# Sparse attention's compression ahead of the norms, four ada_w units at other steps, and 128 rows in the scan's decays product

## The chip, the cores and the metric

The kernel runs on one core of a Trainium2 chip, as one program. The metric is the device time of one execution in microseconds. Everything is computed in float32. A core has a matrix engine (TensorE, PE), a vector engine (VectorE, DVE), an engine for activations (ScalarE, ACT), a small general one (GpSimd, POOL) and SyncE (SP), whose queue issues the weight loads here. Each runs its own list of instructions in order, and they wait for each other by semaphores. Weights come from HBM by DMA into SBUF; TensorE writes into PSUM.

## What is computed

The reference is one block of a hybrid model (short convolution, native sparse attention, gated delta rule, then a two-level mixture of experts) followed by two blocks with modulation (MLA with a feed-forward part, a state-space mixer with a mixture of experts), for 256 tokens of width 1024. What matters here are three pieces of it:

```python
def nsa_compress(kv, pe, w1, w2):            # keys and values of the compressed branch
    idx = jnp.arange(n_cmp)[:, None] * CMP_STRIDE + jnp.arange(CMP_LEN)[None, :]
    blocks = kv[:, idx] + pe[:, None, :]
    flat = jnp.moveaxis(blocks, 3, 2).reshape(b, n_cmp, g, CMP_LEN * d)
    return jax.nn.gelu(flat @ w1) @ w2

q = rms_norm(u_q.reshape(b, s, g, hpg, d), qk_gain[0])
k_c = rms_norm(nsa_compress(kv[:, :, 0], ...), qk_gain[1])
k_s = rms_norm(kv[:, :, 2], qk_gain[2])
k_w = rms_norm(kv[:, :, 4], qk_gain[3])

mod = cond @ ada_w[i] + ada_b[i]             # modulation, 6144 columns for each of two layers

a_cs = jnp.cumsum(dt * a)                    # the scan: decays of 32 heads over the tokens
decay = jnp.exp(a_t[..., :, None] - a_t[..., None, :])
```

The compression takes the first 256 columns of the key and value projection as they are, without a norm. The modulation rows depend on nothing but `cond`, and the first layer's are used long after the attention.

## The kernel before

**Weights.** A weight matrix is cut into units of up to 2 MB (4096 columns of a [128, 4096] float32 tile). `Ring` holds four slots. SyncE issues the loads in the order in which the units were added, and a load waits until the unit four places before it is no longer needed (`emptied`). The order of `columns_unit`, `gate_unit`, `branch_unit` and `ada_units` in `block` is therefore the order of the DMA queue. An ada_w pair is two units, 4 MB, and gives 1024 columns of modulation.

**Split weights.** Most units are multiplied in three passes (high by high, high by low, low by high). `Split` cuts a unit into parts of [128, 1024]: ScalarE casts a part to its high half (`make_hi`, L192), VectorE subtracts it from the ring's to get the low half (`make_lo`, L202), TensorE multiplies (L257 to L259). There are four part buffers, so part n can be cast only when part n-4 has been multiplied. The last low half of a unit frees its ring slot. The ada_w and cmp units are multiplied straight from the ring, and TensorE frees them.

**PSUM.** Four pairs of banks are taken in turn (`banks.take`), each freed by whoever reads it out; `hold` keeps a pair out of the turn.

**The stages in question.** `gdn_*` is the delta rule, at whose end TensorE makes AU, then waits for VectorE's `o`, then transposes it (oT). `nsa_*` follows. Its TensorE list is: the products of the three nsa units (queries; 512 columns of keys and values; 256 more), ada_w pairs 3, 4 and 5, each a product of 64 matmuls (`ada_pe`, L1086) that ScalarE copies (`ada_act`), TensorE turns (`ada_turn_pe`) and VectorE stores (`ada_turn_dve`); then, when all the norms are done, the transposes of q (nqT) and keys (nkT); the transposes of dup (kcT), a doubled copy of the unnormed keys and values; then, from `fl` (the shifted blocks plus `cmp_pe`, 16 instructions of VectorE, L1803), the compression product of 128 matmuls (L1663), its gelu (h1, h2, h1T) and second product (kc), with steps of `gate (2,0)` between. Then `attention_pe` runs 12 jobs with more gate and branch steps beside them. When the stage is over (`finished(s, S["nsa"])` in `sync`), the first expert weights are issued.

VectorE in this stage: the low halves, `nsa_norm_dve` three times (squares, sums, a wait for GpSimd's power, two or three multiplications a half), dup (L1791), the ada stores, `fl`.

**The scan.** `csT` holds the running sums of 32 heads, one a row. For each head `decays_pe` (L3097) multiplies a column of `ident`, broadcast to 128, by `csT`, which puts row h on all 128 partitions. Two of them stand ahead of the loop of `ssm_pe` and one in each of its steps but the last two, in front of the step's part of the x or z projection.

Of the kernel before, what the change touches and what calls it, by code (L numbers as in the profile page):

```python
# [13 lines left out]
ACT = mybir.ActivationFunctionType  # L14
AX = mybir.AxisListType

P = 128
# [318 lines left out]
def block(nc, A, out):  # L336
# [5 lines left out]
    def sb(name, shape, dt=F32, where=None):  # L342
        return (where or ctx).enter_context(nc.sbuf_tensor(name, shape, dt))
# [247 lines left out]
    csT = sb("csT", [32, T], where=sm)  # L591
# [58 lines left out]
    def branch_unit(r, half):  # L650
        columns_unit(("branch", r, half), w_branch[r], 512 * half, 512, row_parts(512, 4))
# [5 lines left out]
    branch_unit(0, 1)  # L657
    columns_unit(("nsa", 0), w_in, O_Q, 512, row_parts(512))
    columns_unit(("nsa", 1), w_in, O_KV, 512, row_parts(512))
    columns_unit(("nsa", 2), w_in, O_KV + 512, 256, row_parts(256))  # L660
    gate_unit(2, 0)
    ada_units(0, 3, ADA_PAIRS)
# [3 lines left out]
    gate_unit(2, 1)  # L666
    branch_unit(2, 1)
# [596 lines left out]
    def gdn_pe(p):  # L1264
# [95 lines left out]
        ins.then_inc(*e.up("AU"))  # L1360
        p.wait_ge(*st.dve.of("o"))
# [3 lines left out]
    def gdn_act(a):  # L1365
# [49 lines left out]
        banks.empty(e, "ST")  # L1415

# [215 lines left out]
    def nsa_pe(p):  # L1632
# [12 lines left out]
        for h0 in (0, 4):  # L1645
            ps = banks.take(p, "nqT", h0)
            transposes(p, ps, [q[:, t, 64 * h:64 * h + 64] for h in range(h0, h0 + 4) for t in range(NT)]).then_inc(*e.up("nqT", h0))
        ps = banks.take(p, "nkT")
        transposes(p, ps, [kv[:, t, 256 + 256 * b + 64 * gr:256 + 256 * b + 64 * gr + 64]
                           for b in range(2) for gr in range(2) for t in range(NT)]).then_inc(*e.up("nkT"))  # L1650
# [16 lines left out]
        ada_turn_pe(p, 0, 5)  # L1667
        merge_step_pe(p, 2, 0)
# [3 lines left out]
        merge_step_pe(p, 2, 1)  # L1672
# [17 lines left out]
    def nsa_act(a):  # L1690
# [11 lines left out]
        for n in range(3, ADA_PAIRS):  # L1702
            ada_act(a, 0, n)
# [7 lines left out]
        a.wait_ge(*st.pe.of("kcT"))  # L1711
        a.copy(kcT[:, :, :].rearrange("p h t -> p (h t)"), banks.of("kcT")).then_inc(*e.up("kcT"))
        banks.empty(e, "kcT")
        a.wait_ge(*st.pe.of("cmp"))
        a.copy(h1, banks.of("cmp")[:, 0:P]).then_inc(*e.up("h1"))
        banks.empty(e, "cmp")
        merge_step_act(a, 2, 0)
        a.wait_ge(*st.dve.of("h2"))
        a.activation(h2, h2, ACT.Sigmoid, scale=2.0 * math.sqrt(2.0 / math.pi)).then_inc(*e.up("h2"))
        a.wait_ge(*st.pe.of("h1T"))  # L1720
        a.copy(h1T[:, :, :].rearrange("p n c -> p (n c)"), banks.of("h1T")[:, 0:P]).then_inc(*e.up("h1T"))
        banks.empty(e, "h1T")
# [13 lines left out]
        merge_step_act(a, 2, 3)  # L1736
        attention_act(a, st, nsa_s, nsa_pT, nsa_mx, nsa_den, 1.0, nsa_jobs, beside=merge_beside_act)
# [4 lines left out]
    def nsa_norm_dve(v, buf, c0, n, gain, scale, k0):  # L1742
# [5 lines left out]
        for t in range(NT):  # L1748
            settle(v, v.tensor_reduce(rn[:, t, k0:k0 + n], w[:, t, :].rearrange("p (n d) -> p n d", d=64), AX.X, ADD),
                   d, "squares", k0)  # L1750
        v.wait_ge(*st.pool.of("rn", k0))
# [26 lines left out]
    def nsa_dve(v):  # L1778
# [13 lines left out]
        ada_turn_dve(v, 0, 3)  # L1792
        ada_turn_dve(v, 0, 4)
# [11 lines left out]
        ada_turn_dve(v, 0, 5)  # L1805
# [4 lines left out]
        merge_step_dve(v, 2, 0)  # L1810
# [9 lines left out]
        attention_dve(v, st, nsa_s, nsa_mx, nsa_den, 1.0, nsa_jobs, nsa_score, nsa_finish, beside=merge_beside_dve)  # L1820
        v.wait_ge(*st.act.of("ynT"))
# [1207 lines left out]
    def ssm_pe(p):  # L3029
# [18 lines left out]
        for t in range(NT):  # L3048
            ins = p.transpose(ps[:, t * 32:t * 32 + 32], csT[:, t * P:(t + 1) * P], ident[0:32, 0:32])
# [253 lines left out]
    def ssm_dve(v):  # L3303
# [23 lines left out]
        v.memset(on32[:, :], 1.0).then_inc(*d.up())  # L3327
        v.memset(upad2[:, :, :, 0:3], 0.0).then_inc(*d.up("pad"))
# [4 lines left out]
        v.tensor_tensor_scan(csT[:, :], on32[:, :], daT[:, :], 0.0, MUL, ADD).then_inc(*d.up("csT"))  # L3333
# [257 lines left out]
```

## Time and profile before

| | |
|---|---|
| median of 3 runs | 2529.43 us (2526.84 to 2530.2) |
| profiled execution | 2528.53 us, its span 2526.7 us |
| TensorE busy | 2146.5 us, 85% of the span |
| VectorE, ScalarE busy | 1424.3 us (56%), 1157.9 us (46%) |
| DMA | 656.69 MB, mean 260 GB/s |
| mean cast of a part (L192), mean low half (L202) | 1015 ns, 1178 ns |

The profile is one execution with the start and end of each instruction. It is read here in these ways: the chain of work that ended last (who held whom up), the timeline (instructions in order; in brackets the idle time ahead and who ended it), windows (busy time of each engine in a stretch, granted TensorE clock as a share of 2.4 GHz, DMA), waits, and the DMA issues. A float32 matmul appears as two passes or more, and the ends of matmuls are modelled, so distances between starts are the safer measure. In a group of the timeline the second number is its whole length.

### The profile page before, as it was taken

What the parts mean: (1) busy time and instruction counts of PE and PEld (TensorE: products, weight loads), DVE (VectorE), ACT (ScalarE), POOL (GpSimd) and SP (SyncE); (2) the same over time, 40 slices, a digit from 0 to 9 for tenths busy, and PEclk for the clock granted to TensorE, in tenths of its full rate; (3) what the DMA queues carried; (4) which work ended last, traced back from release to release, by engine and by line L of the source; (5) the groups of instructions that cost most, each with busy time, mean ns of one, the idle gap of its engine ahead of it and who ended that gap; (6) DMA issues with size and microseconds to landing.
All of it is one profiled execution on the core that took longest, in us unless ns stands there. A gap on an engine that the chain in (4) does not pass through costs nothing.

```text
span 2526.7 us, 29676 instructions
## 1 busy us (share of the span) xinstructions
PE 2146.5 (85%) x12223; PEld 1622.4 (64%) x12223; DVE 1424.3 (56%) x1976; ACT 1157.9 (46%) x1520; POOL 40.9 (2%) x107
## 2 busy tenths in 40 slices
PE   6889788876656656887999988879999999999997
PEld 6867566652111111566997867668787787887875
DVE  3844435421111101434455666658889888888997
ACT  4432244310000000443443556538777787777775
POOL 0000100000000000000000000000000000000000
PEclk9989898879888888997999888889999999999999
DMA  8451651469999999476445322238989989989994
GB/s 265 167 182 69 234 199 56 178 253 408 409 409 409 409 409 402 165 267 234 151 183 183 112 90 99 84 125 293 362 323 329 373 324 359 339 314 371 332 335 189
DMA packets 267692, 656.69 MB, mean 260 GB/s; under 512 B 13456, under 2 KB 38548, under 8 KB 267546
## 3 DMA queue, kind: packets, MB, share of 16 engines
q1 hardware_dynamic: 266592, 652.90, 69.6%
q8 instruction: 101, 1.65, 0.3%
q10 hardware_dynamic: 952, 1.77, 0.2%
q14 instruction: 47, 0.37, 0.0%
HBM read 653.60 MB, written 1.05 MB: 259 GB/s over the span
## 4 chain that ended last, share of the span: by engine, by line
PE 68%; DMA 16%; DVE 9%; ACT 4%; issue 2%; POOL 0%; ACTq 0%; DVEq 0%; POOLq 0%; SPq 0%
PE psum L257 17%; PE psum L258 17%; PE psum L259 16%; PE psum L252 9%; DMA ring<-in_w_expert_up 5%; DMA ring<-in_w_expert_down 5%; DMA ring<-in_w_expert_gate 5%; PE psum L2344 2%; DVE w_lo L202 2%; PE psum L1086 1%; ACT w_hi L192 1%; PE psum L879 1%; PE psum L2366 1%; DMA ring<-in_ada_w 1%; DVE xbc L885 1%
## 5 line engine op out<-in xcount | busy, mean ns | idle before, releaser
L202 DVE TENSOR_TENSOR w_lo<-ring,w_hi 128x1024 fp32r<-128x1024 f32 (+1 forms) x778 | 905.0, 1178 | 399.7 <-ACT w_hi L192 384.6
L192 ACT CAST w_hi<-ring 128x1024 fp32r<-128x1024 f32 (+1 forms) x778 | 785.2, 1015 | 442.9 <-PE psum L259 438.6
L257 PE MATMUL psum<-w_hi,xg_hi 128*128 128x512 f32 (+1 forms) x768 | 294.7, 384 | 1.3 <-ACT xg_lo L2027 1.3
L259 PE MATMUL psum<-w_lo,xg_hi 128*128 128x512 f32 (+1 forms) x768 | 289.5, 377 | 0.0
L258 PE MATMUL psum<-w_hi,xg_lo 128*128 128x512 f32 (+1 forms) x768 | 289.5, 377 | 0.0
L2344 PE MATMUL psum<-ring,hT 128*32 128x512 f32 x960 | 149.7, 756 | 114.6 <-DMA ring<-in_w_expert_gate 64.8
L2344 PEld LDWEIGHTS psum<-ring,hT 128*32 128x32 f32 x960 | 29.8, 126 | 229.4 <-issue 79.0
L257 PEld LDWEIGHTS psum<-w_hi,xg_hi 128*128 128x128 f32 x768 | 144.8, 189 | 31.1 <-issue 1.7
L258 PEld LDWEIGHTS psum<-w_hi,xg_lo 128*128 128x128 f32 x768 | 144.9, 189 | 29.4 <-issue 1.7
L259 PEld LDWEIGHTS psum<-w_lo,xg_hi 128*128 128x128 f32 x768 | 144.7, 188 | 29.2
L257 PE MATMUL psum<-w_hi,midT_hi 128*128 128x512 f32 x352 | 140.8, 400 | 3.9 <-DVE w_lo L202 3.9
L2196 DVE TENSOR_TENSOR x<-x,psum 128x1024 f32<-128x1024 f32 x14 | 17.1, 1221 | 218.8 <-PE psum L252 218.8
L258 PE MATMUL psum<-w_hi,midT_lo 128*128 128x512 f32 x352 | 139.5, 396 | 0.0
L259 PE MATMUL psum<-w_lo,midT_hi 128*128 128x512 f32 x352 | 139.5, 396 | 0.0
L2366 PE MATMUL psum<-ring,midT 128*32 128x512 f32 x480 | 71.4, 727 | 40.5 <-DMA ring<-in_w_expert_down 40.0
L257 PE MATMUL psum<-h_f_hi,w_hi 128*128 128x256 f32 x352 | 99.1, 282 | 2.0 <-DVE h_f_lo L802 2.0
L258 PE MATMUL psum<-h_f_hi,w_lo 128*128 128x256 f32 x352 | 98.9, 281 | 0.0
L259 PE MATMUL psum<-h_f_lo,w_hi 128*128 128x256 f32 x352 | 98.9, 281 | 0.0
L257 PEld LDWEIGHTS psum<-w_hi,midT_hi 128*128 128x128 f32 x352 | 66.3, 188 | 20.8 <-issue 5.4
L2379 ACT COPY midT<-psum 128x512 f32<-128x512 f32 x8 | 4.7, 585 | 161.5 <-PE psum L879 161.5
L259 PEld LDWEIGHTS psum<-w_lo,midT_hi 128*128 128x128 f32 x352 | 66.3, 188 | 16.1
L258 PEld LDWEIGHTS psum<-w_hi,midT_lo 128*128 128x128 f32 x352 | 66.3, 188 | 15.4
(662 smaller groups left out, 3722.7 us busy)
## 6 DMA issues: line engine op xcount, KB each, us to landing
ring<-in_moe_w_gate SPq DMA_DIRECT2D x40, 2048.0 KB, 9.3
ring<-in_moe_w_up SPq DMA_DIRECT2D x40, 2048.0 KB, 10.0
ring<-in_moe_w_down SPq DMA_DIRECT2D x40, 2048.0 KB, 9.2
ring<-in_w_expert_gate SPq DMA_DIRECT2D x30, 2048.0 KB, 17.5
ring<-in_w_expert_up SPq DMA_DIRECT2D x30, 2048.0 KB, 17.6
ring<-in_w_expert_down SPq DMA_DIRECT2D x30, 2048.0 KB, 17.8
ring<-in_ada_w SPq DMA_DIRECT2D x24, 2048.0 KB, 8.9
ring<-in_ssm_w_in SPq DMA_DIRECT2D x10, 2048.0 KB, 8.0
```

Of the source, the lines that this page charges most:

```text
L192: a.copy(self.buffers(n, src.shape)[0], src).then_inc(*self.hi_made.up())
L202: v.tensor_tensor(lo, src, hi.bitcast(F32), SUB).then_inc(*self.lo_made.up())
L252: ins = p.matmul(o, l, r, start=n == 0, stop=n == len(terms) - 1)
L257: p.matmul(o, l[0], r[0], start=start, stop=False)
L258: p.matmul(o, l[1], r[0], start=False, stop=False)
L259: return p.matmul(o, l[0], r[1], start=False, stop=stop)
L879: ins = p.transpose(ps[0:c, n * P:n * P + r], src, ident[0:r, 0:r])
L885: settle(v, v.scalar_tensor_tensor(out_, padded[:, f, j:j + T], w_cols(j), out_, MUL, ADD), st.dve, *name)
L1086: ins = p.matmul(ps[32 * quarter:32 * quarter + 32, 0:256], cond[:, k:k + 1].to_broadcast([P, 32]), w[quarter // 2][:, k, c0:c0 + 256], st ...
L2196: v.tensor_tensor(M.acc[:, t, :], M.acc[:, t, :], run.banks.of(st.name, "scatter", i, t), ADD).then_inc(*st.dve.up("acc", i, t))
L2344: ins = p.matmul(ps[slots_of(j), g * 512:(g + 1) * 512], M.xg[:, 2 * q + k, slots_of(j)], w[:, j, k, :], start=2 * q + k == 0, stop=2 * q ...
L2366: ins = p.matmul(ps[slots_of(j), cut], M.midT[:, q, slots_of(j)], w[:, j, cut], start=q == 0, stop=q == 3)
```

## The change

In the order of units, ada_w pair 3 is loaded ahead of nsa 0, pair 4 ahead of nsa 2, and pair 5 behind gate (2,1). TensorE multiplies pair 3 between AU and oT at the end of `gdn_pe`, pair 4 between nsa 0 and nsa 1, and pair 5 just ahead of the attention jobs; they are turned behind nsa 0, behind kcT, and behind the jobs. On TensorE kcT and the compression product come ahead of the transposes of q and the keys, gate step (2,0) ahead of the compression product and (2,1) behind it. On ScalarE the copies of kcT, h1 and h1T come ahead of those of nqT and nkT. On VectorE the squares are split off the norms (`nsa_squares_dve`) and done between low halves as soon as their columns are there, dup comes ahead of all norms, and the norms of the two keys come behind `fl`; the norm of q stays ahead of it. In the scan, `csT` has 128 rows, set to zero first, and the decays product takes all 128 of them.

```diff
-    csT = sb("csT", [32, T], where=sm)
+    csT = sb("csT", [P, T], where=sm)
@@ order of units
+    ada_units(0, 3, 4)
     columns_unit(("nsa", 0), w_in, O_Q, 512, row_parts(512))
     columns_unit(("nsa", 1), w_in, O_KV, 512, row_parts(512))
+    ada_units(0, 4, 5)
     columns_unit(("nsa", 2), w_in, O_KV + 512, 256, row_parts(256))
     gate_unit(2, 0)
-    ada_units(0, 3, ADA_PAIRS)
     for j in range(2):
         columns_unit(("cmp", j), A["cmp_w1"][0][j], 0, 256)
     branch_unit(2, 0)
     gate_unit(2, 1)
+    ada_units(0, 5, ADA_PAIRS)
     branch_unit(2, 1)
@@ gdn_pe
         ins.then_inc(*e.up("AU"))
+        ada_pe(p, 0, 3)
         p.wait_ge(*st.dve.of("o"))
@@ gdn_act, at its end
+        ada_act(a, 0, 3)
@@ nsa_pe
-        ada_pe(p, 0, 3)
-        ada_pe(p, 0, 4)
-        ada_turn_pe(p, 0, 3)
-        ada_pe(p, 0, 5)
-        ada_turn_pe(p, 0, 4)
-        p.wait_ge(*st.dve.of("normed"))
...
+            if n == 0:
+                ada_turn_pe(p, 0, 3)
+                ada_pe(p, 0, 4)
         p.wait_ge(*st.dve.of("dup"))
         ps = banks.take(p, "kcT")
...
+        ada_turn_pe(p, 0, 4)
+        merge_step_pe(p, 2, 0)
         p.wait_ge(*st.dve.of("fl"))
...
-        ada_turn_pe(p, 0, 5)
-        merge_step_pe(p, 2, 0)
+        merge_step_pe(p, 2, 1)
         p.wait_ge(*st.dve.of("h1"))
         ps = banks.take(p, "h1T")
         transposes(p, ps, [h1]).then_inc(*e.up("h1T"))
-        merge_step_pe(p, 2, 1)
+        p.wait_ge(*st.dve.of("normed"))
+        for h0 in (0, 4):
+            ps = banks.take(p, "nqT", h0)
...
         merge_step_pe(p, 2, 3)
+        ada_pe(p, 0, 5)
         p.wait_ge(*st.act.of("vc"))
         attention_pe(p, st, nsa_s, nsa_pT, nsa_jobs, beside=merge_beside_pe)
+        ada_turn_pe(p, 0, 5)
@@ nsa_act: ada_act(0, 4) behind the copy of nsa 0, ada_act(0, 5) ahead of attention
@@ nsa_dve
-        for n in range(3):
-            split.make_lo(v, min(split.end(unit["nsa", n]) + PARTS, cap))
-        v.wait_ge(*st.act.of("proj", 2))
-        nsa_norm_dve(v, q, 0, 8, gains[:, 0, :], 64.0 ** -0.5, 0)
-        nsa_norm_dve(v, kv, 256, 2, gains[:, 2, :], 1.0, 8)
-        nsa_norm_dve(v, kv, 512, 2, gains[:, 3, :], 1.0, 10)
+        split.make_lo(v, min(split.end(unit["nsa", 1]) + 1, cap))
+        v.wait_ge(*st.act.of("proj", 0))
+        ada_turn_dve(v, 0, 3)
+        nsa_squares_dve(v, q, 0, 8, 0)
+        split.make_lo(v, min(split.end(unit["nsa", 1]) + PARTS, cap))
+        v.wait_ge(*st.act.of("proj", 1))
         for jg in range(4):
             for c in range(2):
                 v.tensor_copy(dup[:, jg, :, 64 * c:64 * c + 64], kv[:, :, 64 * jg:64 * jg + 64]).then_inc(*d.up("dup"))
+        nsa_squares_dve(v, kv, 256, 2, 8)
+        split.make_lo(v, min(split.end(unit["nsa", 2]) + PARTS, cap))
+        nsa_norm_dve(v, q, 0, 8, gains[:, 0, :], 64.0 ** -0.5, 0)
...
+        v.wait_ge(*st.act.of("proj", 2))
+        nsa_squares_dve(v, kv, 512, 2, 10)
+        merge_step_dve(v, 2, 0)
+        ada_turn_dve(v, 0, 4)
+        nsa_norm_dve(v, kv, 256, 2, gains[:, 2, :], 1.0, 8)
+        nsa_norm_dve(v, kv, 512, 2, gains[:, 3, :], 1.0, 10)
@@ decays_pe
-        product(p, ps[:, 0:T], [(ident[0:32, h:h + 1].to_broadcast([32, P]), csT[:, :])]).then_inc(*S["ssm"].pe.up("decay", h))
+        product(p, ps[:, 0:T], [(ident[:, h:h + 1].to_broadcast([P, P]), csT[:, :])]).then_inc(*S["ssm"].pe.up("decay", h))
@@ ssm_dve
+        v.memset(csT[:, :], 0.0).then_inc(*d.up())
...
-        v.tensor_tensor_scan(csT[:, :], on32[:, :], daT[:, :], 0.0, MUL, ADD).then_inc(*d.up("csT"))
+        v.tensor_tensor_scan(csT[0:32, :], on32[:, :], daT[:, :], 0.0, MUL, ADD).then_inc(*d.up("csT"))
```

## Rows read from the trace of the kernel before

**Rows 1.** The page, chain that ended last, share of the span by engine

```profile
PE 68%; DMA 16%; DVE 9%; ACT 4%; issue 2%; POOL 0%; ACTq 0%; DVEq 0%; POOLq 0%; SPq 0%
```

**Rows 2.** Timeline of TensorE, end of gdn to compression: start, length, instructions, [idle before]

```profile
248.75 2.05 PE L252 MATMUL psum<-shared,decT 128*128 128x128 f32 x16 [0.78 <-DVE shared L1478]
258.13 1.97 PE L879 MATMUL psum<-ident,shared 128*128 128x128 f32 x8 [7.32 <-DVE shared L1489]
...
289.24 3.66 PE L1086 MATMUL psum<-ring,cond 128*32 128x256 f32 x64
299.71 5.39 PE L1086 MATMUL psum<-ring,cond 128*32 128x256 f32 x64 [6.82 <-DMA ring<-in_ada_w]
...
311.77 6.18 PE L1086 MATMUL psum<-ring,cond 128*32 128x256 f32 x64 [6.13 <-DMA ring<-in_ada_w]
...
318.35 1.92 PE L879 MATMUL psum<-ident,q 128*64 128x128 f32 x16
...
328.35 6.43 PE L1663 MATMUL psum<-ring,fl 128*32 128x128 f32 x128 [6.34 <-DVE fl L1803]
```

**Rows 3.** Windows: stretch, length, busy PE, PEld, DVE, ACT, POOL (count), clock, DMA, GB/s

```profile
297.60:301.40 3.80, 1.69 (x17) 0.93 (x21) 3.61 (x6) 0.00 (x0) 0.00 (x0) 0.50 1.05 386
328.30:334.70 6.40, 6.35 (x128) 5.74 (x128) 0.00 (x0) 0.00 (x0) 0.00 (x0) 0.56 0.25 92
335.20:350.80 15.60, 15.25 (x66) 10.06 (x65) 5.31 (x10) 5.71 (x13) 0.72 (x2) 1.00 0.89 309
351.00:465.00 114.00, 102.58 (x501) 78.96 (x501) 60.63 (x169) 57.15 (x137) 0.00 (x0) 0.90 0.17 59
575.00:1010.00 435.00, 268.03 (x1643) 79.42 (x1635) 61.17 (x174) 19.48 (x31) 0.35 (x2) 0.85 1.03 408
```

**Rows 4.** SyncE's DMA issues; last, ada_w's size and median us to landing

```profile
211.14 0.37 SPq L139 DMA_DIRECT2D ring<-in_w_in  x1
...
265.56 30.55 SPq L139 DMA_DIRECT2D ring<-in_ada_w  x6
...
464.89 0.92 SPq L128 DMA_DIRECT2D place_ns<-in_w_expert_gate  x2
...
ring<-in_ada_w SPq DMA_DIRECT2D x6, 2048.0 KB, 9.0
```

**Rows 5.** Timeline of VectorE, the filling of fl

```profile
323.19 5.10 DVE L1803 TENSOR_TENSOR fl<-kcT,cols 64x120 f32<-64x120 f32 x16 [4.42 <-ACT kcT L1712]
```

**Rows 6.** Timeline of ScalarE, first cast of nsa 0 and the copies of nqT

```profile
222.76 1.04 ACT L192 CAST w_hi<-ring 128x1024 fp32r<-128x1024 f32 x1 [0.90 <-PE psum L259]
...
319.42 1.91 ACT L1706 COPY hT<-psum 64x1024 f32<-64x1024 f32 x2 [0.47 <-PE psum L879]
```

**Rows 7.** Timeline of TensorE, from kcT2 to the first scores

```profile
345.19 0.21 PE L1680 MATMUL psum<-ident,kc 30*64 30x30 f32 x1 [0.35 <-DVE kc L1817]
...
350.83 1.06 PE L252 MATMUL psum<-kcT,hT 64*128 64x15 f32 x8
```

**Rows 8.** Timeline of TensorE in the first experts

```profile
582.70 3.24 PE L2344 MATMUL psum<-ring,hT 128*32 128x512 f32 x16 [3.19 <-DMA ring<-in_w_expert_gate]
588.44 1.92 PE L2344 MATMUL psum<-ring,hT 128*32 128x512 f32 x16 [2.51 <-DMA ring<-in_w_expert_gate]
```

**Rows 9.** Timeline of TensorE in the scan; last, a wait of its weight loads

```profile
1449.95 2.78 PE L252 MATMUL psum<-xbc 128*128 128x256 f32 x16
1452.48 0.47 PE L257 MATMUL psum<-w_hi,h_ssm_hi 128*128 128x512 f32 x1
...
1480.11 0.69 PE L252 MATMUL psum<-csT,ident 32*128 32x256 f32 x2
1480.74 0.39 PE L257 MATMUL psum<-h_ssm_hi,w_hi 128*128 128x256 f32 x1
...
PEld psum L257 <- issue: 7.9, 22, 0.7
```

**Rows 10.** Timeline of VectorE, the memset of 32 rows

```profile
1413.62 0.27 DVE L3327 MEMSET on<- 32x256 f32 x1
```

More of the change, by code:

```diff
@@ L1638, in nsa_pe @@
             by_token_pe(p, u, h_mix, [[ps[:, t * 512:t * 512 + w] for t in range(NT)]])
-        ada_pe(p, 0, 3)
-        ada_pe(p, 0, 4)
-        ada_turn_pe(p, 0, 3)
-        ada_pe(p, 0, 5)
-        ada_turn_pe(p, 0, 4)
-        p.wait_ge(*st.dve.of("normed"))
[L1645 to L1650, printed above, removed]
+            if n == 0:
+                ada_turn_pe(p, 0, 3)
+                ada_pe(p, 0, 4)
         p.wait_ge(*st.dve.of("dup"))
@@ L1671, in nsa_pe @@
         transposes(p, ps, [h1]).then_inc(*e.up("h1T"))
-        merge_step_pe(p, 2, 1)
+        p.wait_ge(*st.dve.of("normed"))
+        for h0 in (0, 4):
+            ps = banks.take(p, "nqT", h0)
+            transposes(p, ps, [q[:, t, 64 * h:64 * h + 64] for h in range(h0, h0 + 4) for t in range(NT)]).then_inc(*e.up("nqT", h0))
+        ps = banks.take(p, "nkT")
+        transposes(p, ps, [kv[:, t, 256 + 256 * b + 64 * gr:256 + 256 * b + 64 * gr + 64]
+                           for b in range(2) for gr in range(2) for t in range(NT)]).then_inc(*e.up("nkT"))
         p.wait_ge(*st.act.of("h1T"))
@@ L1701, in nsa_act @@
             banks.empty(e, "unit", u)
-        for n in range(3, ADA_PAIRS):
-            ada_act(a, 0, n)
+            if n == 0:
+                ada_act(a, 0, 4)
+        a.wait_ge(*st.pe.of("kcT"))
+        a.copy(kcT[:, :, :].rearrange("p h t -> p (h t)"), banks.of("kcT")).then_inc(*e.up("kcT"))
+        banks.empty(e, "kcT")
+        merge_step_act(a, 2, 0)
+        a.wait_ge(*st.pe.of("cmp"))
+        a.copy(h1, banks.of("cmp")[:, 0:P]).then_inc(*e.up("h1"))
+        banks.empty(e, "cmp")
+        a.wait_ge(*st.dve.of("h2"))
+        a.activation(h2, h2, ACT.Sigmoid, scale=2.0 * math.sqrt(2.0 / math.pi)).then_inc(*e.up("h2"))
+        a.wait_ge(*st.pe.of("h1T"))
+        a.copy(h1T[:, :, :].rearrange("p n c -> p (n c)"), banks.of("h1T")[:, 0:P]).then_inc(*e.up("h1T"))
+        banks.empty(e, "h1T")
         for h0 in (0, 4):
@@ L1710, in nsa_act @@
         banks.empty(e, "nkT")
[L1711 to L1722, printed above, removed]
         merge_step_act(a, 2, 1)
@@ L1736, in nsa_act @@
         merge_step_act(a, 2, 3)
+        ada_act(a, 0, 5)
         attention_act(a, st, nsa_s, nsa_pT, nsa_mx, nsa_den, 1.0, nsa_jobs, beside=merge_beside_act)
@@ L1740, in nsa_act, with nsa_squares_dve @@
         a.copy(ys_[0][:, :, :].rearrange("p f t -> p (f t)"), banks.of("ynT")).then_inc(*e.up("ynT"))
-    def nsa_norm_dve(v, buf, c0, n, gain, scale, k0):
+    def nsa_squares_dve(v, buf, c0, n, k0):
         st = S["nsa"]
@@ L1750, in nsa_norm_dve @@
                    d, "squares", k0)
+    def nsa_norm_dve(v, buf, c0, n, gain, scale, k0):
+        st = S["nsa"]
+        d = st.dve
+        heads = buf[:, :, c0:c0 + 64 * n]
         v.wait_ge(*st.pool.of("rn", k0))
@@ L1791, in nsa_dve @@
                 v.tensor_copy(dup[:, jg, :, 64 * c:64 * c + 64], kv[:, :, 64 * jg:64 * jg + 64]).then_inc(*d.up("dup"))
-        ada_turn_dve(v, 0, 3)
-        ada_turn_dve(v, 0, 4)
+        nsa_squares_dve(v, kv, 256, 2, 8)
+        split.make_lo(v, min(split.end(unit["nsa", 2]) + PARTS, cap))
+        nsa_norm_dve(v, q, 0, 8, gains[:, 0, :], 64.0 ** -0.5, 0)
         v.memset(fl[:, :, :, 30:32], 0.0).then_inc(*d.up("fl"))
@@ L1804, in nsa_dve @@
                                         pe_cols.unsqueeze(2).to_broadcast([64, 8, 15]), ADD).then_inc(*d.up("fl"))
-        ada_turn_dve(v, 0, 5)
+        v.wait_ge(*st.act.of("proj", 2))
[4 more added lines that the diff above has]
+        nsa_norm_dve(v, kv, 512, 2, gains[:, 3, :], 1.0, 10)
         v.wait_ge(*st.act.of("h1"))
@@ L1809, in nsa_dve @@
         v.tensor_tensor(h2, h2, h1, MUL).then_inc(*d.up("h2"))
-        merge_step_dve(v, 2, 0)
         v.wait_ge(*st.act.of("h2"))
@@ L1820, in nsa_dve @@
         attention_dve(v, st, nsa_s, nsa_mx, nsa_den, 1.0, nsa_jobs, nsa_score, nsa_finish, beside=merge_beside_dve)
+        ada_turn_dve(v, 0, 5)
         v.wait_ge(*st.act.of("ynT"))
@@ L3048, in ssm_pe @@
         for t in range(NT):
-            ins = p.transpose(ps[:, t * 32:t * 32 + 32], csT[:, t * P:(t + 1) * P], ident[0:32, 0:32])
+            ins = p.transpose(ps[:, t * 32:t * 32 + 32], csT[0:32, t * P:(t + 1) * P], ident[0:32, 0:32])
         ins.then_inc(*e.up("cs"))
```

## The prediction

> **What bounds the kernel now.** I read the page first. The chain that ended last is mostly TensorE (68%), with DMA second (16%) [rows 1]; so a change pays only where TensorE stands still or works at length on that chain. The change touches two places, and I read each as a timeline, engine by engine.
>
> The first is the sparse-attention stage. Behind oT (258.13) TensorE multiplies the three nsa units and is through at 289.24. Then it does little for 46 us: it waits 6.82 and 6.13 us for ada_w to land, works on both at a low clock, waits another 6.34 us for VectorE to fill `fl`, and runs the compression product at 0.56 of full clock [rows 2, 3]. The cause shows in the DMA issues: all six ada_w units are issued from 265.56 on, in one block [rows 4], and the cmp units stand behind them. VectorE meanwhile does everything ahead of `fl`: squares and norms of q and both keys (q's norm is the stretch of 3.8 us at 297.6 [rows 3]), then dup, up to 310.3, and only then `fl` at 323.19, 5.1 us long [rows 5]. `fl` also waited for kcT, which was transposed behind nqT and nkT, whose copies ScalarE makes first [rows 2, 6]. Attention starts at 350.83 [rows 7].
>
> Is what is gained here kept? The first expert weights are issued at 464.89 [rows 4], when the stage is over, and the experts then run at the pace of DMA: TensorE waits 3.19 and 2.51 us before one quarter unit and another, and the stretch from 575 to 1010 moves 408 GB/s [rows 3, 8]. That stream is started by the end of the attention stage and by what follows it, and nothing in it has a time of its own. An earlier end shifts all of it, one for one.
>
> The second place is the state-space scan. There one step of about 4.28 us is 24 matmuls, 6 small ones and one decays product, with no gap of TensorE between them. This product (two passes, 32 rows) begins at 1480.11 and the next matmul at 1480.74: 0.63 us [rows 9].
>
> **The change, part by part, sparse attention.** I lay the new order out in the times of the trace of before.
>
> ada unit pair 3 goes in between AU (from 248.75, 2.05 us) and oT (258.13), where TensorE sat idle for 7.32 us [rows 2]. At full clock such a product of 64 matmuls is 3.66 us, at low clock up to 6.18 [rows 2]; either fits, so it costs nothing; without that cover it would cost 3.7. The idle left is 3.5 us. Gaps of 3.19 us were followed by a slow quarter, gaps of 2.51 by a fast one [rows 8], so I credit no clock gain to the next stage. Its weights take the ring places in front of nsa 0 and 1, so nsa 0 is now issued when nsa 2 was, at 211.14 [rows 4], and nsa 1 one unit later. nsa 0 is first cast at 222.76, and a 2 MB unit of ada_w took 9.0 us to land beside others [rows 6, 4]: 2.6 us of slack, counted as nothing.
>
> Nsa 0 ends at 272.2 (my reading from its 48 matmuls, 289.24 less 5.8 and 11.2). Behind it come turn 3 (0.5) and ada pair 4 (3.7), loaded from 255 on into an idle queue. So nsa 1 ends at 287.6 and nsa 2 at 293.4, 4.2 later than now. The casts of ScalarE and its copy that empties the bank of nsa 0 both fall under ada 4.
>
> VectorE: the squares of q, dup and the squares of the first keys now lie in the gaps between the w_lo parts (one of 1.2 us to each 2.8 us of TensorE) while nsa 1 and 2 are multiplied. The last part of gate (2,0) can be cast only when nsa 2 is done: a cast and a w_lo of the page's mean, 1.0 and 1.2 (table above) with the hand-overs, give 295.8. Then q's norm, still ahead of `fl`: 3.8, 299.6. kcT is transposed at 293.4, copied by 296.1, so no wait. `fl` 5.2 with its hand-over: done at 304.9. It was 328.3 [rows 2]: **23.4 us earlier**. TensorE does kcT (0.9), turn 4 and gate step (2,0) (2.8) in that time and then idles 7 us, so I leave the compression product at its slow 6.4 us [rows 2]: done at 311.3.
>
> From there: gate step (2,1) 2.8 (12 matmuls of 512 columns at 0.23), h1T 0.3, nqT and nkT 2.6 (moved in here; from 318.35 to 320.97 before [rows 2]), kc 0.8: 317.8. Gate step (2,2) ends at 320.6. ScalarE must first copy h1T, nqT twice and nkT (1.0 each [rows 6]), so the cast of step 1 is at 318.1 to 319.2, then the kc copies, the next cast, its w_lo on VectorE to 322.1, and kc's norm to 322.7: TensorE idles 2.1 us, a new wait (0.35 before [rows 7]). From kcT2 to the first scores 5.64 us, as before (345.19 to 350.83) [rows 7]: 328.4. Then ada pair 5, put before attention: its loads are issued when the compression product frees their slots, at 311.3, and take two units of at most 9 us each in the worst case, 5.1 at the stream's rate; landed by 323 or, at the outside, 330. At the full clock that TensorE had here from 335.2 to 350.8 [rows 3], 3.7: **scores start at 332.1, 18.7 us earlier.** If it runs at low clock, or lands last, 16.
>
> In the attention itself nothing else is added. gate (1,0) now needs the slot of gate (2,1), freed some 13 us into attention, and by 9 us a unit lands about 22 us in, just when its first part was to be cast; ScalarE has over 2 us to spare there. I count 0, with 2 us as the far end. Turn 5 (0.5) and its copy fall where TensorE waits for yn. The order in which the PSUM banks turn is the same in attention, shifted by one. So the stage brings -18.7 us; ends -12 (2 us each lost at nsa 0, `fl` and gate (1,0)) and -23.
>
> **The scan.** The rows 32 to 127 that are added are zeros in csT, and ident is zero there in the columns used, so the result is unchanged and the number of instructions too. What a 128-row pair of this shape costs is to be seen in cb's product: 16 passes, 8 of 256 columns and 8 of 128, in 2.53 us from 1449.95 to 1452.48, with no gap to the next matmul [rows 9]. That is 0.21 for a pass of 256, 0.42 a pair, against 0.63: 0.2 us saved per decays product. The weight loads tell why: after a decays pair the next load stood 0.36 us (22 times, 7.9 in all) for nothing that the profile shows [rows 9]. There are 32 products; 30 stand in the loop, and some 22 to 24 of them in stretches where TensorE has no gap. 23 x 0.2 = **-4.5 us**. Ends: 0, and 32 x 0.25 = -8. The memset adds some 0.3 us to VectorE (the 32-row `on` took 0.27 [rows 10]) where it waits for ScalarE's casts anyway, nothing on the path.
>
> The Trainium skill has two rules that pull apart here. Its page "TensorE: Matmul & The Clock Gate", section "Why this matters for your kernels", says that a single matmul of 32 rows takes the same time as one of 128; by that the padding brings nothing. Its page "TensorEngine Tiling (Array Packing)", section "Key Properties", says that a change of the tiling mode drains the engine; by that each decays product in a stream of 128-row matmuls pays twice. The row of 0.63 against 0.42 stands with the second.
>
> Sum: 18.7 + 4.5 = 23.2. The profiled execution took 2528.5 us with a span of 2526.7; less 23.2 it is 2505.3. The median of the runs shown is 2529.4, 0.9 above, so I predict 2506.2.
>
> **The rivals.** (a) *The padding brings nothing*, because the wait is in the weights and not in the rows: 2529.4 - 18.7 = 2510.7. For: the load before the pair is short already. Against: the 0.63. (b) *A wait takes the place of part of the gain in attention*: `fl` comes later than I lay it out, because VectorE is now asked for more between nsa 1 and nsa 2, or ada 5 lands late behind the compression product. 5 to 9 us lost: 2511 to 2515. (c) *More is gained*: the compression product at full clock (-2.5), no new wait at kcT2 (-2), fewer slow matmuls at 260 and 300: 2498 to 2501. (d) *Slower*: the two idle gaps close together (7 us at 297.6, 2.1 us at 320.6) leave TensorE at 1.2 GHz into attention, where before it ran at 2.4 GHz from 335.2 to 350.8 and at a mean of 0.91 through attention [rows 3]. A 512-column matmul takes 0.43 instead of 0.23; the stage from 351 to 465 has 102.6 us of TensorE work, so all of it at the lower level costs over 50 us, and from half of it on the change is slower: 2506 + 30 = 2536 for a little over half. Against: gaps of 2.5 us left the clock alone [rows 8], and after a wait of 6.34 us and the compression product TensorE had its full clock back at 335.2 [rows 3]. (e) *No change*: the gain stops at the expert stream; it would need a DMA that starts by itself, and none does: 2529.
>
> **How the numbers follow.** The forecast 64%, (a) 10%, (b) 12%, (c) 7%, (d) 4%, (e) 3%. The forecast's own range is 2501 to 2510. To hold 8 in 10 the range takes in (a), most of (b) and part of (c): 2498 to 2515. A measurement tells 0.2%, 5 us, from no change; faster 0.93, same 0.03, slower 0.04.
>
> **What would show it.** Right: AU followed by 64 ada matmuls and no ada_w wait of TensorE after 289; `fl` done near 305; one wait of about 7 us ahead of the compression product; scores from 332; the first expert issue near 446; decays pairs followed by the next matmul after 0.42 us. Wrong: a DMA wait in ada 5 or a ScalarE wait for gate (1,0), a granted clock under 0.8 between 325 and 350, or decays pairs still 0.63.

## The result and the profile after

The changed kernel takes **2493.67 us** (median of 4 runs, 2492.2 to 2503.84), the kernel before beside it 2529.81 (4 runs): a ratio of 0.9867, 95% interval 0.9839 to 0.9895. Two later comparisons gave 0.987 and 0.988; over all three its 12 runs have a median of 2495.6 us (2492.05 to 2503.97). The forecast was 2506.2 with a range down to 2498. The sign and the two mechanisms held, and more was gained than I allowed for: 2493.67 lies below the range. The profiled execution took 2494.8 us, its span 2493.1: 33.6 less than before.

The page's chain of the changed kernel by engine. DMA fell from 16% to 15% [rows 1], and TensorE's two waits for ada_w in this stage are gone:

```profile
PE 67%; DMA 15%; DVE 10%; ACT 5%; issue 2%; POOL 0%; ACTq 0%; DVEq 0%; POOLq 0%
```

Timeline of TensorE in the changed kernel, the lines that answer to [rows 2, 7]. (After's line numbers: L1086 is L1088 now, L879 L881, L1663 L1660, L1680 L1682.)

```profile
249.16 2.05 PE L252 MATMUL psum<-shared,decT 128*128 128x128 f32 x16 [0.78 <-DVE shared L1482]
251.15 3.66 PE L1088 MATMUL psum<-ring,cond 128*32 128x256 f32 x64
258.54 1.27 PE L881 MATMUL psum<-ident,shared 128*128 128x128 f32 x8 [3.74 <-DVE shared L1493]
...
272.67 3.66 PE L1088 MATMUL psum<-ring,cond 128*32 128x256 f32 x64
...
304.73 6.50 PE L1660 MATMUL psum<-ring,fl 128*32 128x128 f32 x128 [7.11 <-DVE fl L1814]
...
314.18 1.91 PE L881 MATMUL psum<-ident,q 128*64 128x128 f32 x16
...
322.22 0.21 PE L1682 MATMUL psum<-ident,kc 30*64 30x30 f32 x1 [1.58 <-DVE kc L1832]
...
327.87 3.66 PE L1088 MATMUL psum<-ring,cond 128*32 128x256 f32 x64
331.46 1.06 PE L252 MATMUL psum<-kcT,hT 64*128 64x15 f32 x8
```

The three ada_w products run at full clock, 3.66 us each, with no wait in front. The compression product starts at 304.73 instead of 328.35, the scores at 331.46 instead of 350.83. The queue of SyncE, and VectorE's and ScalarE's lines in the same place:

```profile
254.87 0.99 SPq L139 DMA_DIRECT2D ring<-in_ada_w  x2
...
311.30 0.99 SPq L139 DMA_DIRECT2D ring<-in_ada_w  x2
...
444.77 0.92 SPq L128 DMA_DIRECT2D place_ns<-in_w_expert_gate  x2
```
```profile
299.64 5.03 DVE L1814 TENSOR_TENSOR fl<-kcT,cols 64x120 f32<-64x120 f32 x16
```
```profile
315.25 1.92 ACT L1722 COPY hT<-psum 64x1024 f32<-64x1024 f32 x2 [0.61 <-PE psum L881]
...
319.48 1.03 ACT L192 CAST w_hi<-ring 128x1024 fp32r<-128x1024 f32 x1
```

`fl` has no wait in front any more (4.42 us for kcT before [rows 5]). Its end is set by VectorE's own work, with q's norm as the last piece of it. The first expert issue is 20.1 us earlier than before [rows 4].

The scan, timeline of TensorE, and the waits of the weight loads in the same stretch, to be set beside [rows 9]:

```profile
1459.58 0.78 PE L252 MATMUL psum<-xs,hT 128*128 128x64 f32 x6
1460.20 0.65 PE L252 MATMUL psum<-csT,ident 128*128 128x256 f32 x2
1460.50 0.47 PE L257 MATMUL psum<-h_ssm_hi,w_hi 128*128 128x256 f32 x1
```
```profile
PEld psum L257 <- issue: 1.5, 1, 1.5
```

From the start of the decays pair to the next matmul it is 0.30 us, where it was 0.63, and of the 22 unexplained waits of the weight loads one is left.

**Where the time went.** I cut both executions at the same instructions (starts of TensorE's matmuls, and the issue of the first expert weights), and took the lengths between. These are differences of starts in the timelines, not lines of the profile:

| stretch, us | before | after | difference |
|---|---|---|---|
| start to the first expert issue | 464.9 | 444.8 | -20.1 |
| to the first expert matmul | 83.4 | 77.5 | -5.9 |
| first experts, to MLA | 464.9 | 467.2 | +2.3 |
| MLA and feed-forward, to the first decays product | 445.1 | 445.5 | +0.4 |
| scan | 161.4 | 154.3 | -7.1 |
| scan's end to the second experts | 83.3 | 80.1 | -3.2 |
| to the end | 823.7 | 823.7 | 0 |

The two edited places give 27.2 us. The other 6.4 come from stretches in which the change altered nothing but the small memset of csT on VectorE, in the fourth. The forecast had 23.2 for the two places and nothing for the rest. Not every stretch is as steady as its row: over all profiles the scan, with one and the same code in it, took either 161.3 to 161.5 or 163.4 to 163.6 us with 32 or 64 rows, and either 154.1 to 154.6 or 156.4 with 128.

### The profile page after: what moved, and what is told of

It is laid out like the page before. It is cut to its first block, busy times and chain, and to the rows that moved or that the text cites. A ratio compares the mean times of both kernels' runs of the same rounds, so it can differ in the third digit from the quotient of the medians.

```text
span 2493.1 us, 29680 instructions
## 1 busy us (share of the span) xinstructions
PE 2128.2 (85%) x12223; PEld 1615.8 (65%) x12223; DVE 1424.0 (57%) x1977; ACT 1158.1 (46%) x1520; POOL 43.5 (2%) x107
## 4 chain that ended last, share of the span: by engine, by line
PE 67%; DMA 15%; DVE 10%; ACT 5%; issue 2%; POOL 0%; ACTq 0%; DVEq 0%; POOLq 0%
PE psum L257 17%; PE psum L259 16%; PE psum L258 16%; PE psum L252 8%; DMA ring<-in_w_expert_down 5%; DMA ring<-in_w_expert_up 5%; DMA ring<-in_w_expert_gate 5%; PE psum L2360 2%; DVE w_lo L202 2%; ACT w_hi L192 1%; PE psum L1088 1%; PE psum L2382 1%; PE psum L881 1%; DVE xbc L887 1%; PE psum L2071 1%
## 5 line engine op out<-in xcount | busy, mean ns | idle before, releaser
L257 PEld LDWEIGHTS psum<-w_hi,xg_hi 128*128 128x128 f32 x768 | 144.8, 188 | 31.1 <-issue 1.7
L258 PEld LDWEIGHTS psum<-w_hi,xg_lo 128*128 128x128 f32 x768 | 144.8, 189 | 29.4 <-issue 1.7
```

Source lines behind the costliest of these rows:

```text
L257: p.matmul(o, l[0], r[0], start=start, stop=False)
L258: p.matmul(o, l[1], r[0], start=False, stop=False)
```

## The experiments

None of the kernels leaves out or alters a part of the computation. Two theories stood at the start: **clock** (the two halves of the change are worth some 19 and 7 to 9 us, they add, and what is left over is TensorE's granted clock, which differs from one execution to the next in stretches that nobody edited) and **strengthening** (an earlier attention stage really makes what follows faster, so that the whole is more than its parts). Beside them: whether the attention edits need each other, and what the padding of the decays product pays for.

**1 and 2. Each half alone.** The attention edits with the old scan, and the scan's edit with the old attention:

```diff
# attention only: everything of the change but
-    csT = sb("csT", [P, T], where=sm)
+    csT = sb("csT", [32, T], where=sm)
-        product(p, ps[:, 0:T], [(ident[:, h:h + 1].to_broadcast([P, P]), csT[:, :])]) ...
+        product(p, ps[:, 0:T], [(ident[0:32, h:h + 1].to_broadcast([32, P]), csT[:, :])]) ...
# scan only: the kernel before with the four edits of csT, decays_pe, ssm_dve and the transposes of csT
```

> The changed kernel with the scan put back to 32 rows; the attention part is whole. By my ledger of the two traces the scan's loop brings 7 to 9 us (0.33 us for each of some 25 decays products), so this should take 2501 to 2503 us. By the prediction's price of 0.2 us a product it would be 2498. The first expert weights should be issued at 444.8 us, as in the changed kernel. If the 5.8 us that the stretch from that issue to the first expert matmul gained (83.4 to 77.6 us) belongs to the kernel's timing, it is 77.6 again here, since everything ahead of it is the same; if the clock there falls out differently at each execution, it will differ.

> The kernel before with the scan part of the change alone. Ledger: 7 to 9 us less, 2521 to 2523; by the prediction's price 4.5 less, 2525; by 'a matmul of 32 rows costs what one of 128 costs', no change. From the start of a decays pair to the next matmul 0.30 us instead of 0.62, and 0.33 less from step to step.

Measured: attention alone 2511.27 us (2505.91 to 2513.5), ratio 0.9929 [0.9912, 0.9945]; the scan alone 2519.71 (2517.22 to 2522.77), ratio 0.9961 [0.9947, 0.9975]. That is 17.8 and 9.3 us less than the 2529.04 of before beside them; the sum, 27.1, is 9 short of the 36.1 between the medians of the first comparison. Attention alone took 8 us more than the 2501 to 2503 expected, the scan alone a little less than its 2521 to 2523. The scan alone has its stretch at 154.2 us, 7.2 shorter, like the whole. Attention alone issues the first expert weights at 442.3, as early as the whole, but has 83.4 us from there to the first expert matmul, as before. Up to the scan its code is that of the changed kernel, which took 77.5.

**3 and 4. The two attention edits apart.** First the new order of the norms, kcT and `fl`, with the six ada_w units left in one block; then the ada_w units spread, with the old order:

```diff
# order only
-    ada_units(0, 3, 4)
     columns_unit(("nsa", 0), w_in, O_Q, 512, row_parts(512))
...
     gate_unit(2, 0)
+    ada_units(0, 3, ADA_PAIRS)
# spread only: the ada_w units as in the change, and in nsa_pe
+        p.wait_ge(*st.dve.of("normed"))
+        ... nqT, nkT ahead of kcT, and in nsa_dve the three whole norms ahead of dup
```

> The changed order inside the stage (kcT and the compression product ahead, squares early), but all three ada_w pairs loaded and multiplied in one block behind the nsa units, as before; scan as before. If the two edits need each other: TensorE comes to kcT only when pair 5 has landed, near 318.5 us, fl is ready near 325.5 (before 328.3), and what is moved behind the compression product takes that back, so 1 to 3 us less than before, 2527 to 2529. If each edit brings its own part, about 10 us less, 2520.

> The ada_w pairs at the new places in the queue and on TensorE, but norms, nqT and nkT ahead of kcT and the compression as before; scan as before. If the two edits need each other: nothing waits for ada_w any more, but the chain of norms and copies now sets the end; fl near 323.5 us, then ada pair 5 (3.7 us) ahead of attention, so 1 to 3 us less than before, 2527 to 2529. If each edit brings its own part, about 10 us less, 2520.

Measured: 2525.8 us for the order alone, ratio 0.9986 [0.9971, 1.0], and 2525.27 for the spread alone, 0.9987 [0.9976, 0.9999]. Some 3 to 4 us each by the medians, with intervals that touch or nearly touch no change (at the first expert issue of their profiles 3.0 and 0.7 us), where the two together bring 18 to 20. Both came out a little under the 2527 to 2529 expected if the two need each other, and well above the 2520 expected if each brings its own part. Timeline of TensorE, order alone:

```profile
300.11 5.34 PE L1086 MATMUL psum<-ring,cond 128*32 128x256 f32 x64 [6.93 <-DMA ring<-in_ada_w]
312.01 6.21 PE L1086 MATMUL psum<-ring,cond 128*32 128x256 f32 x64 [6.02 <-DMA ring<-in_ada_w]
325.99 3.70 PE L1658 MATMUL psum<-ring,fl 128*32 128x128 f32 x128 [3.06 <-DVE fl L1810]
```

and spread alone:

```profile
312.69 3.62 PE L881 MATMUL psum<-ident,q 128*64 128x128 f32 x16 [19.52 <-DVE kv L1762]
324.44 6.42 PE L1666 MATMUL psum<-ring,fl 128*32 128x128 f32 x128 [6.27 <-DVE fl L1809]
340.82 0.21 PE L1682 MATMUL psum<-ident,kc 30*64 30x30 f32 x1 [0.35 <-DVE kc L1822]
```

With the block left in place the two DMA waits stay. With it gone, and the norms still first, TensorE stands idle for 19.52 us behind VectorE: the transfers had hidden VectorE's work, and VectorE's work the transfers. Whoever removes one finds the other.

**5. The whole again,** on another chip, for its own scatter.

> The changed kernel itself once more, beside the kernel before. If the two parts simply add and the rest of what its first profile showed (5.8 us between the first expert issue and the first expert matmul, 3.2 us behind the scan) is the granted clock of that execution, its median is that of the attention part alone less 9.3 us: 2499 to 2504, with single runs from 2492 up, and a profile may show 83.4 us again in that stretch. If the two parts strengthen each other, 2492 to 2495 again.

Measured: 2495.25 us (2492.05 to 2500.35), ratio 0.987 [0.9851, 0.9889]; in its profile 77.5 us from the first expert issue to the first expert matmul, as in the first. That is under the 2499 to 2504 that the clock theory had asked and close to the 2492 to 2495 of strengthening; experiments 9 to 11 take the question up again.

**6. 64 rows in place of 128,** to learn whether the padding pays by the number of rows or by bringing the product into the shape of its neighbours.

```diff
-    csT = sb("csT", [P, T], where=sm)
+    csT = sb("csT", [64, T], where=sm)
-        product(p, ps[:, 0:T], [(ident[:, h:h + 1].to_broadcast([P, P]), csT[:, :])]) ...
+        product(p, ps[:, 0:T], [(ident[0:64, h:h + 1].to_broadcast([64, P]), csT[:, :])]) ...
```

> The changed kernel with csT and the decays product at 64 rows instead of 128. If what 32 rows cost is a switch of the array's shape between neighbouring matmuls, 64 rows cost the same: 0.62 us from a decays pair to the next matmul, 4.2 to 4.3 us a step. If it goes by the number of rows, the pair lies between, near 0.5 us. If only 32 rows are slow, 0.30 us.

Timeline of TensorE in the scan with 64 rows:

```profile
1461.59 0.69 PE L252 MATMUL psum<-csT,ident 64*128 64x256 f32 x2
1462.22 0.38 PE L257 MATMUL psum<-h_ssm_hi,w_hi 128*128 128x256 f32 x1
```

It is 0.63 us again, as with 32 rows, the weight loads have their 22 unexplained waits of 7.9 us in all back, and the scan's stretch is 161.5 us. One execution took 2509.93 us, within the range of the attention edits alone. So doubling the rows bought nothing, and filling all 128 bought everything. The price does not go by the row; it fits one paid where products of a part of the rows stand among products of all of them, which is a reading and not shown by itself: no run puts two such products side by side at full clock, or tries another number of rows.

**7. q's norm behind `fl`.** In the changed kernel q's norm, 3.8 us, is the last thing ahead of `fl` and on the path.

```diff
         split.make_lo(v, min(split.end(unit["nsa", 2]) + PARTS, cap))
-        nsa_norm_dve(v, q, 0, 8, gains[:, 0, :], 64.0 ** -0.5, 0)
...
         nsa_norm_dve(v, kv, 512, 2, gains[:, 3, :], 1.0, 10)
+        nsa_norm_dve(v, q, 0, 8, gains[:, 0, :], 64.0 ** -0.5, 0)
```

> The changed kernel with the norm of q (3.8 us of VectorE) behind fl and the keys' norms too. fl begins at 296 us instead of 299.7 and is ready at 301; TensorE's wait ahead of the compression product falls from 7.1 to 3.3 us. If VectorE is what sets this stretch, the scores start 3 to 4 us earlier, near 328, and the time falls by as much. If the norm then comes late for nqT behind the compression product, the gain is under 1.5 us.

Measured: 2493.47 us (2487.37 to 2499.61), ratio 0.9846 [0.9829, 0.9864], against 0.987 [0.9851, 0.9889] for the change on that chip; the intervals overlap. Timeline of TensorE:

```profile
302.39 5.00 PE L1660 MATMUL psum<-ring,fl 128*32 128x128 f32 x128 [3.60 <-DVE fl L1813]
...
311.66 0.33 PE L881 MATMUL psum<-ident,nsa_s 128*128 128x128 f32 x1 [1.27 <-DVE nsa_s L1827]
...
319.86 0.21 PE L1682 MATMUL psum<-ident,kc 30*64 30x30 f32 x1 [1.57 <-DVE kc L1832]
```

The wait in front of the compression product is 3.60 instead of 7.11. The product itself ran partly at full clock here and took 5.00 us, not 6.50, but 1.27 us of new wait follow it: h1's gelu stands behind q's norm on VectorE. In experiment 12, with the same order, the product took 6.46 us and this wait is missing; the two make up for each other. The scores are at 329.1, 2.4 us earlier, where 3 to 4 were expected.

**8. Work for TensorE in its gaps.** Between the attention and the experts TensorE stands still three times for longer (4.43, 6.12 and 6.67 us in the first profile); behind the last two it works mostly at the lower clock (in the kernel before 0.61 in the mean of the 34.9 us ahead of the first expert matmul, both gaps among them). Four, six and six matmuls of 512 columns on constants, whose results nobody reads, go into these gaps (`warm_pe`, called in `proj_pe` and twice in `moe1_pe`):

```diff
+        ps = banks.take(p, "warm", name)
+        for n in range(times):
+            ins = p.matmul(ps[:, 0:512], ident[:, :], ones[:, 0:1].to_broadcast([P, 512]), start=True, stop=True)
+        ins.then_inc(*st.pe.up())
+        banks.empty(st.pe, "warm", name)
```

> The changed kernel with matmuls that compute nothing of use in three gaps of TensorE between attention and the experts (4, 6 and 6 of 512 columns, each some 0.9 us at full clock, in gaps of 4.4, 6.1 and 6.7 us). If the two lengths of that stretch, 83.4 and 77.6 us, differ by when the clock falls and comes back in those gaps, it is 77.6 us or less in every profile, and the median is 3 to 8 us under that of the changed kernel. If the gaps have nothing to do with it, the median is the same or later by what the added matmuls stick out.

Measured: 2491.32 us (2486.13 to 2495.16), ratio 0.9842 [0.9827, 0.9858], 3.9 us under the change on that chip, with intervals that overlap. The stretch to the first expert matmul is 76.3 us, 1.2 less than in the best of the other executions.

**9 to 12. The whole and its halves once more, side by side,** and both tries in one kernel. They decide between the two theories, which the first eight had left open.

> The changed kernel once more, on the same chip and in the same rounds as its two halves below. Theory 'the halves add, and the granted clock decides the rest': the three kernels have the same code between the attention and the scan as each other's parts, so the time saved here is the sum of the savings of the two halves to within 3 us. Theory 'the halves strengthen each other': the saving stays 8 us above the sum, here 35 us against 18 and 9. Both expect 2492 to 2497 us for this kernel; the halves tell.

> The attention edits alone again (the scan's decays as in the kernel before). If the halves add: about 2503 (35 less 9 for the scan: a saving of 26), and in its profile the stretch from the placement's issue to the first expert matmul is 77.6 us rather than 83.4. If they strengthen each other: 2511 again (a saving of 18), with 83.4 us in that stretch.

> The scan edit alone again. 23 products that save 0.33 us each are 7.6 us. If nothing else is in it, 2521 to 2523, with the stretch before the second expert stage at 83.3 us; with that stretch at 80.1 us, 3 us less, 2518 to 2520. Both theories expect a saving of 7 to 11 us.

> Both tries in one kernel: q's norm stands behind fl and the key norms on VectorE, and 4, 6 and 6 matmuls on constants fill three gaps of TensorE between the attention and the experts. Nothing of the computation is left out. Scores 3 us earlier by the first (about 329), the stretch from the placement's issue to the first expert matmul 76.3 to 77.6 by the second. If both are real and add: 2487 to 2490, against 2493 to 2495 for the changed kernel on the same chip. If the granted clock alone made each of them, 2491 to 2495.

| on one chip | us, median | runs | ratio |
|---|---|---|---|
| before | 2529.05 (2523.95 to 2533.76) | 12 | |
| the change | 2497.91 (2495.59 to 2503.97) | 4 | 0.988 [0.9861, 0.9899] |
| attention alone | 2509.03 (2501.25 to 2515.18) | 6 | 0.9918 [0.99, 0.9936] |
| scan alone | 2519.64 (2517.16 to 2522.38) | 6 | 0.9965 [0.9953, 0.9976] |
| both tries | 2488.66 (2484.73 to 2491.4) | 5 | 0.9837 [0.9823, 0.9851] |

Here the halves save 20.0 and 9.4 us, and the whole 31.1: a sum of 29.4, apart by 1.7, well inside the scatter of the runs. Over all chips the medians are 2495.6 (12 runs), 2509.8 (10), 2519.65 (11) and 2529.2 (45 of before): 33.6 against 19.4 + 9.6 = 29.0. On the one chip the whole, at 2497.91, is a microsecond above the 2492 to 2497 that both theories had expected. The whole and the attention alone scatter by 4.3 us from run to run (standard deviation), so the 4.6 between are about two of their uncertainty (4.3 us over the root of 12, and of 10, are 1.2 and 1.4). By the means instead of the medians the whole saves 32.8 and the halves 20.3 + 9.8 = 30.1, and 2.7 are left. Attention alone also had the longer scan, 163.4 and 163.6 us against 161.4 before, in both of its profiles; that is 2 us outside its edits. **Strengthening is not needed, though a few microseconds of it are not excluded.** My guess for attention alone, 2503, missed; 83.0 us stood in the stretch for which the clock theory had asked 77.6. That theory is right in that either length occurs with the same code, and was wrong in tying it to the change.

The profiles show it directly. First the same code, the change, in two executions: windows (stretch, length, busy PE, PEld, DVE, ACT, POOL with counts, granted clock, DMA share, GB/s) of the first profile,

```profile
322.50:335.00 12.50, 12.50 (x101) 7.71 (x100) 2.02 (x7) 4.43 (x15) 0.00 (x0) 1.00 0.35 126
335.00:400.00 65.00, 61.00 (x295) 46.09 (x293) 39.29 (x108) 34.31 (x88) 0.00 (x0) 0.95 0.36 130
400.00:445.00 45.00, 37.41 (x194) 29.77 (x194) 20.27 (x57) 21.52 (x41) 0.00 (x0) 0.83 0.14 47
```

and of experiment 9:

```profile
322.50:335.00 12.50, 12.50 (x77) 5.34 (x75) 1.22 (x1) 0.18 (x1) 0.00 (x0) 0.59 0.23 85
335.00:400.00 65.00, 61.00 (x296) 47.30 (x296) 36.78 (x102) 36.39 (x97) 0.00 (x0) 0.92 0.36 130
400.00:445.00 45.00, 40.21 (x210) 30.59 (x208) 22.62 (x67) 21.44 (x42) 0.00 (x0) 0.92 0.14 47
```

Experiment 9's timeline of TensorE in that place, with the ada_w product that the change put in front of the scores:

```profile
325.52 0.63 PE L258 MATMUL psum<-w_hi,h_mix_lo 128*128 128x512 f32 x1
...
329.78 5.18 PE L1088 MATMUL psum<-ring,cond 128*32 128x256 f32 x64
334.90 1.06 PE L252 MATMUL psum<-kcT,hT 64*128 64x15 f32 x8
```

Its compression product began 1.2 us earlier than in the first profile (303.57), its scores 3.4 later. TensorE was busy throughout and waited for nobody, yet for some 10 of these 12.5 us it had the lower of its two clocks (0.59 in the mean), and the ada_w product took 5.18 us instead of 3.66. Experiments 6 and 10 have the same (scores at 334.6 and 335.8), experiments 1, 5 and 8 do not (330.6, 332.1, 331.9). In the three with the fall the compression product began at 303.2 to 304.5, in the four without it at 304.7 to 305.4; that names no cause.

Then the stretch behind the scan, in the scan alone, twice the same code: windows of experiment 2 and of experiment 11.

```profile
1613.50:1696.70 83.20, 68.16 (x308) 56.82 (x308) 46.41 (x89) 32.53 (x43) 4.76 (x8) 0.85 0.38 133
```
```profile
1612.90:1692.90 80.00, 65.09 (x309) 54.60 (x308) 46.42 (x89) 32.61 (x43) 4.76 (x8) 0.89 0.39 138
```

The same matmuls (one record is missing in the first), VectorE, ScalarE and GpSimd busy for the same time to a tenth of a microsecond, and 3.2 us between them: granted clock 0.85 and 0.89.

**The version that beats both.** q's norm behind `fl` together with the filled gaps: 2488.66 us, a ratio of 0.9837 whose interval does not touch that of the change on the same chip, 9.3 us faster than it and 40.4 than before. Windows of the stretch in front of the first expert matmul, first the kernel before, then the change in its first profile, then this kernel, each cut at the same instructions:

```profile
513.40:548.30 34.90, 19.22 (x96) 18.36 (x96) 14.05 (x52) 8.42 (x14) 3.04 (x22) 0.61 0.61 240
```
```profile
491.50:522.30 30.80, 15.17 (x92) 14.38 (x90) 13.97 (x52) 8.42 (x14) 3.04 (x22) 0.67 0.70 272
```
```profile
488.10:517.70 29.60, 24.19 (x116) 17.14 (x114) 14.02 (x52) 8.42 (x14) 3.04 (x22) 0.88 0.72 284
```

The stretch goes from 34.9 us at a clock of 0.61 to 30.8 at 0.67 and 29.6 at 0.88. VectorE, ScalarE and GpSimd do the same in all three (the longer busy time of TensorE in the third is the added matmuls), and the change in experiment 9 had 34.7 us at 0.61. In the profile of this last version the stretch of MLA and feed-forward took 448.7 us, where the profiles without added matmuls have 442.7 to 446.0; whether that belongs to the added matmuls is not shown.

## Why the prediction was right or wrong

**The attention: right in its steps and nearly in its size.** Predicted -18.7 at the scores, and the expert issue at about 446; the first profile has -19.4 (331.46 against 350.83) and 444.8. Over the three profiles of the change the scores stand at 331.5, 332.1 and 334.9, where 332.1 was forecast. Point by point: AU is followed by 64 ada matmuls, 3.66 us in all, and an idle of 3.74 (3.5 said, though 7.32 less 3.66 is 3.66); no ada_w wait is left; q's norm ended at 299.5 (299.6 said) and `fl` at 304.7 (304.9); the wait ahead of the compression product is 7.11 us (7); that product ran slow, 6.50 (6.4); the cast of step 1 began at 317.97 (318.1), the new wait in front of kcT2 is 1.58 us (2.1). The attention itself, from scores to expert issue, took 113.3 us, 114.1 before, so gate (1,0) lost nothing. Laying the new order out in the times of the old trace, engine by engine, was worth the work.

**The scan: mechanism right, the term mis-sized.** The step that failed is "0.21 for a pass of 256, 0.42 a pair, against 0.63: 0.2 us saved per decays product", times 23 = -4.5. The stretch measured -7.1 (-7.2 and -6.8 in experiments 2 and 11), 0.31 for each of 23. (0.63 less 0.42 is 0.21, and 23 times that 4.8; the 4.5 is rounded down.) Two things were wrong. The price of a pass was taken from cb's product by sharing its 2.53 us out by columns, 0.21 to a pass of 256 and half of it to one of 128; the padded pair gives way to the next matmul after 0.30 us, not 0.42. Shared out evenly the 16 passes take 0.16 each, 0.32 a pair, much nearer. And I counted only what stood behind the pair. From the start of the six xs matmuls in front of it to the pair it was 0.70 us (they began at 1479.41, the pair of [rows 9] at 1480.11), and it is 0.62 now (1459.58 to 1460.20). A whole step of the loop went from 4.28 us to 3.94: 0.09 of it in front of the pair, 0.33 at the pair, and 0.08 given back, since the matmul behind it now gives way after 0.30 us and not 0.22. The row of idle weight loads, 22 times and 7.9 us in all, was in front of me, and I used it as a reason but not as a measure. The far end given, -8, held.

**Added up, with the rest at zero: the failed assumption.** "Sum: 18.7 + 4.5 = 23.2" took the profiled execution of before as it stood outside the edits. Of the 12.5 us between forecast and result, 1.4 lie ahead of the first expert issue, 2.6 in the scan, 6.4 in stretches whose code did not change (-5.9 and -3.2, +2.3 and +0.4), and 2.0 in how each kernel's profiled run stood to its median (0.9 below for before, 1.1 above for after). The 6.4 need no cause in the change: 83 or 77.5 us, and 83.3 or 80.0, occurred with one and the same code. The profile of before shows both stretches at the longest length seen in any profile, so they could hardly but become shorter. That was to be read beforehand, from the clock of 0.61 in front of the first expert matmul; I looked there only at the expert stream, and my range had no term for it. That these 6.4 us fell my way in the first profile is luck; nobody had forecast them.

**The rivals.** (a), the padding brings nothing: refuted by experiments 2 and 11, and its reason too: with 128 rows the unexplained waits of these weight loads are gone. The rule of the Trainium skill that I set against it ("TensorEngine Tiling (Array Packing)", "Key Properties": a change of the tiling mode drains the engine) agrees with the 0.63 us at 32 and at 64 rows, both in a stream of 128. The other ("TensorE: Matmul & The Clock Gate", "Why this matters for your kernels": a single matmul of 32 rows takes as long as one of 128) does not carry over to a product inside this stream, by 0.63 against 0.30. (b), a wait that eats part: 1.58 us at kcT2, already in the sum. (c), more is gained: it came out in the size, 2498 to 2501 said and 2493.7 to 2497.9 measured, but of its three reasons (compression product at full clock, no wait at kcT2, fewer slow matmuls) none did in the profiles of the change: 6.33 to 6.51 us, 1.58 us, and behind oT the matmuls are slow until 262.6 as before (262.4). The gain lay elsewhere. (d), low clock carried into attention: it exists. In experiments 6, 9 and 10 the clock falls near 322.5 or 323.5 for some 10 us, and the price is 3.4 us and not 30; its place there is behind the 1.6 us of idle, though nothing shows that this idle is its cause. (The mean clock of attention in [rows 3] is 0.90, not the 0.91 said there.) (e), no change: each microsecond gained ahead of the expert stream was kept through it to within some 2 us (464.9 us for the first experts before, and 467.2, 463.7 and 465.2 in the three profiles of the change).

**What stays open.** What decides in an execution which of the two clocks a stretch gets. The long stretch to the first expert matmul had its short form in 3 of the 12 profiles without filled gaps (the change twice, the spread edit alone once), and what tells them apart in advance was not found. Two of the change's three profiles have it and one of the nine others: too few to say whether the change makes it likelier. Nor is it settled that the whole is exactly the sum of its halves (33.6 against 29.0 over all runs, 31.1 against 29.4 on one chip). And of the 9.3 us of the last version, 3 are seen at the scores and 1.2 to 7 in the filled gaps, and the longer stretch of MLA and feed-forward stands against them; how much of each is lasting is not separated.

## What to carry to other kernels

When TensorE waits in one place now for a transfer, now for another engine, lay the order of all engines out anew before moving anything: each of two edits alone was worth 3 to 4 us here, both together nearly 20. Fill the rows of a small product that stands between full ones, if zeros are to be had; here that was 0.3 us each time. And before a sum is made against a profiled run, look for stretches at a low granted clock outside the edit: they are the part of the time that changes by itself, and the range has to hold them.

## What was not expected of the hardware

A product of two passes cost 0.3 us more with 32 or 64 rows than with 128, between products of 128 rows: 0.63 us against 0.30 to the next matmul at the full clock, and 1.12 against 0.63 at the low one. TensorE's granted clock fell from 2.4 to 1.2 GHz for some 10 us within a stretch of unbroken work (0.59 in the mean of 12.5 us, against 1.00) in some executions of a kernel and not in others. Sixteen matmuls of no use, put into three idle gaps, made the stretch around them shorter than any without them, 76.3 us in two profiles against 77.5 to 83.4 in twelve.
